# Modulation products in unsplit fp32 on the four column quarters of the array

## What is computed

```python
s_c = jax.nn.silu(c)
s_cc = jax.nn.silu(c_ctx)[None]
for i in range(DEPTH):
    ml = (s_c @ w_mod[i] + b_mod[i]).reshape(-1, 3, 3, D)
    h = gated_residual(h, ml, 0, swiglu(ada_in(h, norm_g[i, 0], ml, 0), ffn_w_in[i, 0], ffn_w_out[i, 0]), 0.5)
    ...
        mc = (s_cc @ w_mod[i] + b_mod[i]).reshape(-1, 3, 3, D)
```

## Time and profile before

| | |
|---|---|
| median of 3 runs | 3498.28 us (3494.55 to 3510.05) |
| the profiled execution | 3498.12 us |
| its span, first to last instruction | 3496.3 us |
| mean granted TensorE clock | 0.981 |
| PE busy | 3340.3 us (96%) |
| DVE busy | 1829.8 us (52%) |
| ACT busy | 1416.7 us (41%) |
| moved by DMA | 497.13 MB, 142 GB/s on average |

### The profile page before, as it was taken

One profiled execution on the slowest core, in us unless ns is written; L12 is line 12 of the kernel. 1 busy time (PEld: TensorE's weight loads), 2 busy tenths in 40 slices (PEclk: granted clock), 3 DMA queues, 4 the chain that ended last, 5 costly groups with the idle time before them and its releaser, 6 DMA issues.

```text
span 3496.3 us, 44481 instructions
## 1 busy us (share of the span) xinstructions
PE 3340.3 (96%) x17862; PEld 2800.2 (80%) x17862; DVE 1829.8 (52%) x2656; ACT 1416.7 (41%) x1898; POOL 93.1 (3%) x127
## 2 busy tenths in 40 slices
PE   7999979999999979999999999989999999999998
PEld 6888768888887768878888778768888788887797
DVE  6755666757756767753334343463333433344654
ACT  5644535545545435542222233233221322234543
POOL 0000000000000000000000000000000000021000
PEclk9999989999999989999999999999999999999999
DMA  7854426857754427843232222212333223254254
GB/s 242 275 186 158 151 77 199 266 196 258 254 169 152 135 96 229 265 157 97 97 112 99 85 85 85 84 49 97 97 103 103 87 98 110 91 133 100 76 181 156
DMA packets 354902, 497.13 MB, mean 142 GB/s; under 512 B 12658, under 2 KB 223500, under 8 KB 354700
## 3 DMA queue, kind: packets, MB, share of 16 engines
q1 hardware_dynamic: 351052, 483.76, 42.2%
q0 software_dynamic: 3648, 10.54, 1.4%
HBM read 493.16 MB, written 1.10 MB: 141 GB/s over the span
## 4 chain that ended last, share of the span: by engine, by line
PE 88%; DVE 6%; ACT 2%; issue 2%; POOL 1%; DMA 1%; SPq 0%; DVEq 0%; POOLq 0%; ACTq 0%
PE bank L483 27%; PE bank L484 26%; PE bank L485 26%; PE bank L496 2%; PE bank L498 2%; DVE wlo L1430 1%; PE bank L882 1%; ACT whi L1019 1%; DVE cv L1711 1%; DMA raw<-in_nat_w_qkv_dram 0%; PE bank L616 0%; PE bank L631 0%; POOL small L2174 0%; PE bank L867 0%; POOL small L2179 0%
## 5 line engine op out<-in xcount | busy, mean ns | idle before, releaser
L1430 DVE TENSOR_TENSOR wlo<-raw,whi 128x1024 fp32r<-128x1024 f32 (+1 forms) x926 | 1107.4, 1213 | 1263.4 <-ACT whi L1019 1262.1
L1019 ACT ACTIVATE whi<-raw 128x1024 fp32r<-128x1024 f32 (+1 forms) x926 | 953.3, 1047 | 1249.7 <-PE bank L485 1212.3
L483 PE MATMUL bank<-xTh,whi 128*128 128x256 f32 (+1 forms) x3200 | 1043.5, 326 | 9.4 <-ACT whi L1019 4.1
L484 PE MATMUL bank<-xTl,whi 128*128 128x256 f32 (+1 forms) x3200 | 1039.4, 325 | 0.0
L485 PE MATMUL bank<-xTh,wlo 128*128 128x256 f32 (+1 forms) x3200 | 1039.0, 325 | 0.0
L483 PEld LDWEIGHTS bank<-xTh,whi 128*128 128x128 f32 x3200 | 608.2, 190 | 72.7 <-issue 9.7
L484 PEld LDWEIGHTS bank<-xTl,whi 128*128 128x128 f32 x3200 | 608.4, 190 | 52.4 <-issue 0.5
L485 PEld LDWEIGHTS bank<-xTh,wlo 128*128 128x128 f32 x3200 | 607.8, 190 | 49.0
L483 PE MATMUL bank<-whi,hh 128*128 128x512 f32 x968 | 376.8, 389 | 0.0
L484 PE MATMUL bank<-wlo,hh 128*128 128x512 f32 x968 | 376.6, 389 | 0.0
L485 PE MATMUL bank<-whi,hl 128*128 128x512 f32 x968 | 376.6, 389 | 0.0
(11 more groups left out here) (331 smaller groups left out, 2485.0 us busy)
## 6 DMA issues: line engine op xcount, KB each, us to landing
raw<-in_ffn_w_in_dram SPq DMA_DIRECT2D x176, 1024.0 KB, 5.2
raw<-in_ffn_w_out_dram SPq DMA_DIRECT2D x80, 1024.0 KB, 5.1
raw<-in_w_mod_dram SPq DMA_DIRECT2D x72, 1024.0 KB, 5.2
raw<-in_w_in_dram SPq DMA_DIRECT2D x44, 1024.0 KB, 5.0
raw<-in_ret_w_in_dram SPq DMA_DIRECT2D x24, 1024.0 KB, 5.1
raw<-in_w_branch_dram SPq DMA_DIRECT2D x12, 1024.0 KB, 5.1
raw<-in_nat_w_qkv_dram SPq DMA_DIRECT2D x12, 1024.0 KB, 8.5
raw<-in_ffn_w_out_dram SPq DMA_DIRECT2D x16, 512.0 KB, 3.4
```

The lines of the kernel that those rows point to most:

```text
L483: pe.matmul(ps, lh, rh, start=start, stop=False, skip_group_check=True)
L484: pe.matmul(ps, lh, rl, start=False, stop=False, skip_group_check=True)
L1019: nc.scalar.activation(hi, src, ACT.Copy).then_inc(*e.inc("hi", key, part))
L1430: nc.vector.tensor_tensor(lo, src, hi.bitcast(F32), ALU.subtract).then_inc(*e.inc("lo", key, part))
```

## The change

- The modulation weights are no longer slabs. They go to four buffers of their own, `mraw` (4 x [128, 4, 512], in room that the FFNs' hidden values leave free), by loads of their own that SP issues behind fixed slabs; each waits for the product four back.
- They are not split. PE multiplies in plain fp32, a half being four matmuls, one for each k-tile, each on another quarter of the array's columns (output partitions 32j to 32j + 31, same bank).
- Three products make a batch: `scp` holds the two vectors amid zero columns, and a window of 32 of them puts the product m on rows 2m and 2m + 1 of each quarter, so that all of a batch adds up in one bank, bank 7. The FFNs with products use the other seven.
- Once per batch (12 times in place of 36) ACT copies the bank to `modrow`, PE adds the four quarters and turns them in one step by four fp32 matmuls with the matrix `sel` of 6 columns, and DVE adds the bias.
- Batches are spread over seven FFNs: 1, 2, 2, 1 in the four of block one, and 2 each in `g1` and `g2` of layer 0 and `g1` of layer 1. So 18 of 36 products move to block two. The gate rows are made in `g1` of each layer.
- `modrow`, `gcol` and `grow` lie in `vgain`, whose own load now waits for the first turn of the layer.

```diff
+MOD_BATCHES = {("f1", 0): (0,), ("f2", 0): (1, 2), ("f1", 1): (3, 4), ("f2", 1): (5,),
+               ("g1", 0): (6, 7), ("g2", 0): (8, 9), ("g1", 1): (10, 11)}
+MOD_POINTS = {1: (9, 13, 17, 21, 25, END), 2: (8, 10, 12, 14, 16, 18, 20, 22, 24, 26, 28, END),
+              512: (2, 3, 4, 5, 6, 7, 9, 9, 10, 11, 12, 13)}
...
-                if mod0 is not None and 0 < g <= MODS_PER_FFN:
-                    mod(mod0 + g - 1, half)
...
+        mraw = [arena(f"mraw{i}", [P, 4, 512], o * KB) for i, o in enumerate((28, 36, 72, 80))]
...
+                    for q in mods.loads.get(s, ()):
+                        name = mods.halves[q][4]
+                        if q >= NMOD:
+                            sp.wait_ge(*e.at("modk", q - NMOD))
+                        if name not in (("f1", 0), ("f1", 1), ("g1", 0)) and q < mods.first[name] + NMOD:
+                            sp.wait_ge(*e.at("turn", name, KD - 1))
+                        sp.dma_start(mraw[q % NMOD][:, :, :], mods.halves[q][3]).then_inc(mod_landed[q % NMOD], 16)
...
-                for part in range(2):
-                    wh, wl = split_ready(("mod", i, half), part)
-                    for j in range(2):
-                        k = 4 * half + 2 * part + j
-                        pe.matmul(ps[0:4, :], sc4[:, k, :], wh[:, j, :], start=k == 0, stop=False,
-                                  skip_group_check=True)
-                        m = pe.matmul(ps[0:2, :], sc4[:, k, 0:2], wl[:, j, :], start=False, stop=k == KD - 1,
-                                      skip_group_check=True)
...
+                pe.wait_ge(mod_landed[q % NMOD], 16 * (q // NMOD + 1))
+                for j in range(4):
+                    pm = pe.matmul(ps[32 * j:32 * j + 32, :], scp[:, 4 * half + j, 4 - 2 * m:36 - 2 * m], mraw[q % NMOD][:, j, :],
+                                   start=m == half == 0, stop=m == BATCH - 1 and half == 1, skip_group_check=True)
...
-                    m = pe.transpose(ps[:, 4 * c:4 * c + 4], modrow[0:4, c * P:(c + 1) * P], ident[0:4, 0:4])
-                m.then_inc(*e.inc("modtp", i))
+                    m = pe.matmul(ps[:, 6 * c:6 * c + 6], modrow[:, c * P:(c + 1) * P], sel, start=True, stop=True)
+                m.then_inc(*e.inc("modtp", b))
...
+                    if t == 0 and name in PREVIOUS:
+                        mod_rows(PREVIOUS[name], END)
...
+            def mod_rows(name, at):
+
+                if (name, at + 1) in mods.turns:
+                    b = mods.turns[name, at + 1]
...
+                    act.wait_ge(*e.at("modp", b))
+                    if b:
+                        act.wait_ge(*e.at("modtp", b - 1))
+                    A(modrow[:, :], unit("modp", b)[:, :], ACT.Copy).then_inc(*e.inc("modrow", b, frees=("modp", b)))
...
+                pool.wait_ge(*e.at("modtp", 4 * l))
                 pool.dma_start(vgain[:, :], wide_row(w["gm_v_norm"][l], 512)).then_inc(L.sem("vgain_landed"), 16)
```

More of the change, by code:

```diff
@@ L135, in add, with __init__ @@
         self.items.append((key, src, kt, n, len(pieces)))
+class Modulation:
+    def __init__(self, slabs, w):
+        self.halves, self.uses, self.loads, self.turns, self.first, self.last = [], {}, {}, {}, {}, {}
+        for name, batches in MOD_BATCHES.items():
+            wide = name[0][0] == "g"
+            points = MOD_POINTS[512 if wide else len(batches)]
+            first = slabs.index[name, "gate", 0]
+            self.first[name], n = len(self.halves), 0
+            for b in batches:
+                for m in range(BATCH):
+                    l, g = divmod(BATCH * b + m, 18)
+                    for half in range(2):
+                        q, at = len(self.halves), points[n]
+                        src = w["w_mod_2"][l][512 * half:512 * half + 512, 512 * g:512 * g + 512]
+                        self.halves.append((b, m, half, src.rearrange("(k p) n -> p k n", p=P), name))
+                        self.uses.setdefault((name, at), []).append(q)
+                        if wide:
+                            ahead = 3 if n < NMOD else at - 1
+                        else:
+                            ahead = 28 if at == END else max(6, at - (4 if len(batches) == 1 else 2))
+                        self.loads.setdefault(first + ahead, []).append(q)
+                        n += 1
+                self.turns[name, at + 1] = b
+            self.last[name] = len(self.halves) - 1
 def plan(w):
@@ L143, in rows, with ffn @@
         return m[k0 * P:(k0 + kt) * P, c0:c0 + n].rearrange("(k p) n -> p k n", p=P)
[L145 to L149, removed]
+    def ffn(name, w_up, w_down):
         for g in range(GROUPS):
@@ L223, in build @@
     slabs = plan(w)
+    mods = Modulation(slabs, w)
     with ExitStack() as ctx:
@@ L471, in new @@
             def new(*key, ring=ALL):
-                u = ring[L.units[ring] % len(ring)]
-                L.units[ring] += 1
+                turn = ALL if ring is SEVEN else ring
+                u = turn[L.units[turn] % len(turn)]
+                L.units[turn] += 1
+                if u not in ring:
+                    u = turn[L.units[turn] % len(turn)]
+                    L.units[turn] += 1
                 L.bank_of[key] = u
@@ new lines, in mod_turn, with mods_at @@
+            def mod_turn(b):
+                if b == 0:
+                    pe.wait_ge(*e.at("sel"))
+                pe.wait_ge(*e.at("modrow", b))
+                ps = new("modtp", b, ring=MODS)
+                for c in range(4):
+                    m = pe.matmul(ps[:, 6 * c:6 * c + 6], modrow[:, c * P:(c + 1) * P], sel, start=True, stop=True)
+                m.then_inc(*e.inc("modtp", b))
+            def mods_at(name, at):
+                if (name, at) in mods.turns:
+                    mod_turn(mods.turns[name, at])
+                for q in mods.uses.get((name, at), ()):
+                    mod(q)
@@ L512, in split_ready, with mod_left @@
+            def mod_left(name):
+                if (name, END + 1) in mods.turns:
+                    mod_turn(mods.turns[name, END + 1])
             def split_ready(key, part):
@@ L1100, in ffn @@
                         act.wait_ge(*e.at("ht", name, g, i))
-                        if name == ("g1", 0) and g + i == 0:
-                            act.wait_ge(L.sem("gate_rows_written"), 16 * DEPTH)
+                        if T == 512 and name in MOD_BATCHES and g == 7 and i == 0:
+                            act.wait_ge(*e.at("modk", mods.last[name]))
                         A(hh[:, o:o + 512], sg[:, b, :], ACT.Copy).then_inc(*e.inc("hhi", name, g, i))
-                    if mod0 is not None and 0 < g <= MODS_PER_FFN:
-                        ahead(until, ("mod", mod0 + g - 1, 1))
+                    mod_rows(name, 2 * g + 1)
+                    if g == 9 and name in GATES_OF:
+                        l = GATES_OF[name]
+                        act.wait_ge(*e.at("growp", l))
+                        A(grow, unit("growp", l)[0:48, 0:P], ACT.Copy).then_inc(*e.inc("grow", l, frees=("growp", l)))
                 for n in range(2):
@@ L1563, in ffn @@
                         parameters(g)
+                    mod_columns(name, 2 * g)
                     ahead(until, (name, "up", g))
```

191 lines of the change are left out of this document (100 added, 91 removed).

## The result

| | before | after |
|---|---|---|
| median | 3498.28 us (3491.81 to 3510.05, 15 runs) | 3478.99 us (3469.51 to 3498.44, 15 runs) |

The account below looks back on a forecast made before the run. PE (TensorE) was taken to bound the kernel, full in the FFNs. Products and turns would cost 92 us in place of 149, gaining 57: 3498 - 57 = 3441 us, range 3423 to 3480.

Parts of the forecast that it names:

- A half, 1.13: Four fp32 quarter matmuls on PE: 0.86 overlapped, 0.02 staggered starts, 0.25 layout change; 72 halves cost 81 us.
- A turn, 0.9: Four fp32 matmuls of 6 columns on PE, 8 records, 0.9 us each; 12 turns cost 11 us.
- In order: Rival: PE's queue passes no waiting record, so a half takes 2.40 us; 3533 us, slower; chance 0.07.
- two at a time: Rival: four fp32 streams cannot be fed at once, so a half takes 1.97 us; 3502 us, the same; chance 0.08.
- no overlap: Rival: matmuls on quarters do not overlap at all, 3.44 us for a half; 3608 us; chance 0.04.
- Lead lost: Rival: at the 12 turns PE waits for ACT's row copy and splits behind it, 25 us; 3466 us; chance 0.07.
- The four products at a stage's end, 0.9 each: At FFN ends ACT's row copy delays the following work 0.9 us, where 1.13 was counted; no correction.
- Splits, POOL's load, seven banks: Fewer ACT and DVE splits, POOL's later value-gain loads and seven banks in place of eight change the time by nothing.
- The rest of the edits: Step pricing removed splits, row copy on ACT, added loads, POOL's loads, seven banks and products at FFN ends: no correction.

Follow-up runs that it names:

- the pairs: The aligned kernel with halves issued two by two, 36 visits to the column quarters in place of 72: 3447.21 us, ratio 0.9849.
- the one-quarter kernel: The changed kernel with only the last quarter's matmul issued in five of six halves, so products are incomplete: 3476.52 us, ratio 0.9948.
- the run with 64 bytes: The kernel before with 64 bytes left free ahead of xTh, so xTh, xTl and the arena begin 64 bytes later: 3526.24 us, ratio 1.0083.
- the aligned kernel: The changed kernel with aff (64 bytes) moved into free columns of cols, so xTh and the arena begin 64 bytes earlier: 3465.03 us, ratio 0.9906.

## Why the prediction was wrong

The mechanism of the products was right and the terms for them held; the total missed costs that the prediction put at nothing, or did not have.
- **A half, 1.13:** 1.19 to 1.20 measured. The fp32 matmul's two passes (0.86) are confirmed by the pairs, whose second half adds 0.85, and the full overlap of the quarters by the one-quarter kernel; the change of layout is 0.33 in place of 0.27 (0.25 and 0.02 for staggered starts), within the bound of 0.39 (1.25 less 0.86). 72 halves: 86 us, not 81.
- **A turn, 0.9:** 0.90.
- **In order, two at a time, no overlap:** all fall, with the one-quarter kernel and the narrow stretches. The Trainium skill, "TensorE: Matmul & The Clock Gate", section "The mechanism", whose strict first in, first out was the first of these: by it, as the prediction applied it to the two records of an fp32 matmul, four of them on quarters would take 2.4 us, and here they take 1.2 with the layout; the measurement decides.
- **Lead lost:** falls. PE never waits for the row copy or a modulation load; its waits for `wlo` are 14.6 us in 4 times, where before had 16.4 in 4.
- **The four products at a stage's end, 0.9 each:** right. From the last down matmul to the next stage's first slab matmul before has 5.34 us three times (248.23 to 253.57 the first time) and 9.57; after has 6.53 (216.41 to 222.94), 6.17, 6.28 and 10.48. That is 1.2, 0.8, 0.9 and 0.9 late, 3.9 in all where 3.6 were taken.
- **Splits, POOL's load, seven banks:** nothing, as said. The value gain was loaded at 236.0 and first used at 313.2.
- **The step that failed** is "The rest of the edits": it prices the queues, the splits and the banks at nothing and has no term for tiles that are made smaller, added and dropped. In the kernel these lines read as housekeeping, yet they move xTh and the arena by 320 bytes. By the run with 64 bytes that is 28.5 us of the missing 38; with it undone, the FFNs of the aligned kernel give 56 where the forecast, counted by stages, has 61. The other 9 are about one long fall of the clock in the mixers (6 to 8), for which the prediction has no term either, and the 5 by which the halves are dearer; that is 2 to 4 more than is missing, which stays open.
- **The range** (3423 to 3480) held the time by 1 us, which is luck: its upper part was there for the lead lost, which did not happen.

## What to carry to other kernels

When a change resizes or adds on-chip tiles, write down the byte addresses of the operands of the hottest matmuls before and after, and keep the distance between the streamed and the stationary operand as it was (here: a multiple of 256 bytes); in a kernel that TensorE fills, a move of 64 bytes cost 0.8%, and it took back half of what the change had earned. To find such a loss compare counts of instructions in equal, full stretches at the same clock, since no wait shows it. Work that needs a narrow stationary operand pays on column quarters, four for one, and more with two halves in one visit than with one, since a visit costs 0.33 us (longer visits were not tried).

## What was not expected of the hardware

- The rate of full-array matmuls depends on the distance of their operands in SBUF modulo 256 bytes: with 512 columns 226.7 to 227.1 ns apart at 0, 229 to 233 at 64, 232.5 to 232.9 at 128. At 64 the steps repeat in a pattern of 226, 229 to 230 and 232 in gate and up. Distances of 192 were not tried, and the cause inside the chip is not shown.
- With 256 columns the odd distance of 64 is the faster one, 117.5 to 117.7 ns against 119.9 (119.4 at 128).
- Four fp32 matmuls of 512 columns on the four column quarters take 1.06 us, and one alone 1.05.
- Going into and out of the quarters costs 0.33 us: 0.09 ahead, 0.11 behind, the rest inside.
- After a wait of 10 us and a return to full clock, TensorE's clock can fall to half once more for 31 us while PE is busy for 27 of them, in one execution and layer and not in another of the same kernel.
